# A mixture of experts: the first expert's rows by a product on TensorE, and the second expert's weights halved during routing

## What is computed

```python
scores = jax.nn.softmax((t @ w_router).astype(jnp.float32), axis=-1)
sel = scores + router_bias
...                       # best group of four, then the best two experts in it
combine = jnp.sum(jax.nn.one_hot(eidx, N_EXPERTS) * wsel[..., None], axis=1)
hg = jnp.einsum('td,edf->tef', t, w_gate)
hu = jnp.einsum('td,edf->tef', t, w_up)
h = jax.nn.silu(hg) * hu * combine[..., None]
y = jnp.einsum('tef,efd->td', h, w_down)
```

## Time and profile before

| | |
|---|---|
| median of 3 runs | 1873.3 us (1868.39 to 1873.57) |
| the profiled execution's own time | 1872.31 us |
| its span | 1870.7 us |
| mean granted TensorE clock | 0.922 of full speed |
| busy PE, DVE, ACT, POOL | 1565.5, 1221.8, 785.7, 738.5 us |
| read from HBM, written | 287.06 MB, 39.44 MB |

### The profile page before, as it was taken

The page is one execution under the profiler, slowest core; times in us unless marked ns, Lnnn a source line. Parts: engine busy times, 40 slices in busy tenths (PEclk is TensorE's granted clock), DMA queues, the critical chain, the costliest instruction groups (busy, mean ns, idle before and its releaser), DMA issues.

```text
span 1870.7 us, 27095 instructions
## 1 busy us (share of the span) xinstructions
PE 1565.5 (84%) x8954; PEld 1338.9 (72%) x8954; DVE 1221.8 (65%) x1662; ACT 785.7 (42%) x1178; POOL 738.5 (39%) x440
## 2 busy tenths in 40 slices
PE   2699899989998975999549989998999988499970
PEld 0589766679997764777438986666999967377750
DVE  0658588878937364777194947887886445477725
ACT  0422577752224132766142247776222413176621
POOL 2124399421114201887212329862111220179941
PEclk7799999999999976999869999999999989599995
DMA  7612165322212642999852205551222262479976
GB/s 289 200 45 68 53 208 203 99 58 80 68 57 91 247 156 110 342 356 338 314 187 74 68 30 181 188 163 36 68 69 78 80 247 83 178 281 353 379 268 235
DMA packets 131206, 310.06 MB, mean 166 GB/s; under 512 B 11636, under 2 KB 81396, under 8 KB 109984
## 3 DMA queue, kind: packets, MB, share of 16 engines
q1 hardware_dynamic: 104096, 224.41, 35.0%
q0 software_dynamic: 16400, 42.90, 6.1%
q10 hardware_dynamic: 10560, 40.90, 5.7%
HBM read 287.06 MB, written 39.44 MB: 175 GB/s over the span
## 4 chain that ended last, share of the span: by engine, by line
PE 62%; DMA 14%; DVE 11%; issue 7%; ACT 4%; POOL 1%; DVEq 0%; ACTq 0%; POOLq 0%; SPq 0%
PE ps L539 26%; PE ps L498 9%; PE ps L800 6%; PE ps L597 3%; PE ps L607 2%; DVE gu_lo L1498 2%; DMA raw_x<-in_w_down 2%; PE ps L454 2%; DMA raw<-in_w_down 2%; PE ps L866 2%; DMA raw<-in_w_up 2%; PE ps L586 2%; DMA raw<-in_w_ada 2%; PE ps L846 2%; PE ps L587 1%
## 5 line engine op out<-in xcount | busy, mean ns | idle before, releaser
L2279 POOL TENSOR_TENSOR w_lo<-raw,w_hi 128x1024 fp32r<-128x1024 f32 (+1 forms) x46 | 162.5, 3535 | 554.9 <-ACT w_hi L1106 554.9
L539 PE MATMUL ps<-u_hi,w_hi 128*128 128x320 f32 x768 | 238.9, 311 | 5.4 <-ACT probs L1205 5.4
L539 PE MATMUL ps<-u_lo,w_hi 128*128 128x320 f32 x768 | 238.1, 310 | 0.0
L539 PE MATMUL ps<-u_hi,w_lo 128*128 128x320 f32 x768 | 238.1, 310 | 0.0
L1106 ACT ACTIVATE w_hi<-raw 128x2048 fp32r<-128x2048 f32 (+1 forms) x64 | 101.3, 1591 | 293.7 <-PE ps L539 133.9
L1853 DVE SCALAR_TENSOR_TENSOR glu<-glu,convw 128x670 f32<-128x670 f32 x164 | 171.1, 1043 | 6.1 <-DVE o_lo L1808 0.6
L539 PEld LDWEIGHTS ps<-u_hi,w_hi 128*128 128x128 f32 x768 | 144.8, 189 | 6.0 <-ACT probs L1205 5.9
L539 PEld LDWEIGHTS ps<-u_lo,w_hi 128*128 128x128 f32 x768 | 144.8, 189 | 0.1
L539 PEld LDWEIGHTS ps<-u_hi,w_lo 128*128 128x128 f32 x768 | 144.8, 189 | 0.0
L2384 POOL DMA_INDIRECT xe<-u_d,tab_u x34 | 68.4, 2012 | 179.6 <-issue 145.2
L1713 DVE TENSOR_TENSOR pt_lo<-ps,pt_hi 128x512 fp32r<-128x512 f32 x160 | 109.7, 687 | 29.9 <-ACT pt_hi L1231 27.8
(11 more groups left out here) (379 smaller groups left out, 4254.2 us busy)
## 6 DMA issues: line engine op xcount, KB each, us to landing
raw<-in_w_ada SPq DMA_DIRECT2D x52, 1024.0 KB, 5.1
raw<-in_w_in SPq DMA_DIRECT2D x48, 512.0 KB, 5.0
raw_x<-in_w_gate SPq DMA_DIRECT2D x16, 1024.0 KB, 7.0
raw<-in_w_up SPq DMA_DIRECT2D x16, 1024.0 KB, 8.3
raw_x<-in_w_down SPq DMA_DIRECT2D x16, 1024.0 KB, 9.2
raw_x<-in_w_up SPq DMA_DIRECT2D x14, 1024.0 KB, 8.6
raw<-in_w_gate SPq DMA_DIRECT2D x14, 1024.0 KB, 6.5
raw<-in_w_down SPq DMA_DIRECT2D x14, 1024.0 KB, 9.2
```

Of the source, the lines that this page charges most:

```text
L539: ins = mm(ps[:, b, 0:HALF], (w_hi, w_lo)[w][:, s, cols(k):cols(k) + P], xs[x][:, k, half * HALF:(half + 1) * HALF], start=(k == 0 and w + ...
L2279: g_.tensor_tensor(w_lo[:, n % 2, 0:k], raw[:, n % 2, 0:k], w_hi[:, n % 2, 0:k].bitcast(F32), ALU.subtract).then_inc(*G.up("g_lo", "w_lo", n))
```

## The change

Expert 0's rows no longer come from the gather. DVE works out each token's place among expert 0's rows (2 x 640 is added where the token does not go to expert 0, so that it matches no place) and compares it with 0 to 127; the comparison matrix, 128 places for each of five tiles of tokens, is multiplied with `u2` on PE, in 8 x 5 products of full precision, into the two PSUM banks in which the transposed rows stood. The place and table products move to banks 6 and 7. `e0_gu` moves to the buffer of the projection weights, and the overflow tiles keep the old one as `over_gu`. The list of units begins with expert 2's gate and up; their high parts are made on ACT and the rests on DVE (gate) and POOL (up) between the last projection and the logits, and expert 1's down weights follow during routing. In the turn of expert 0 nothing is halved any more.

```diff
-GATE_UP_DOWN = [(1, 0), (1, 1)]
-for e in range(NE - 1):
+GATE_UP_DOWN = [(2, 0), (2, 1), (1, 0), (1, 1), (1, 2)]
+for e in range(1, NE - 1):
...
-    e0_gu = at("e0_gu", [P, 2, KC, DE], F32, R_A + 8 * KB)
+    e0_gu = at("e0_gu", [P, 2, KC, DE], F32, R_W)
+    over_gu = at("over_gu", [P, 2, KC, DE], F32, R_A + 8 * KB)
+    e0_sel = at("e0_sel", [P, NT, P], F32, R_A + 60 * KB)
+    e0_pos = at("e0_pos", [P, NT], F32, R_A + 63 * KB)
...
+            for b in range(6):
+                eng.wait_ge(*T.at("drained", last[b]))
+            eng.wait_ge(*T.at("u2", NT - 1))
+            eng.wait_ge(*T.at("e0_sel"))
+            for k in range(KC):
+                for t in range(NT):
+                    ins = mm(ps[:, k // 4, (k % 4) * P:(k % 4 + 1) * P], u2[:, t, k:D:KC], e0_sel[:, t, :], start=(t == 0), stop=(t == NT - 1))
+            ins.then_inc(*T.up("xt_full", "xt_full", 0))
+
             eng.wait_ge(*T.at("at_tile"))
-            b = fill(("table",), 1)
+            b = fill(("table",), 7)
...
-            xe_transposes(0)
...
+            eng.wait_ge(*A.at("filled", ("wo", 1, NT - 1)))
+            hi_expert(UNIT_OF[2, 0])
             ha_tr(NT - 1, 1)
             eng.dma_start(ha_d.rearrange("(t p) d -> p t d", p=P), h_a[:, :, :]).then_inc(*A.up("ha_out", "ha_out", by=16))
             eng.wait_ge(*A.at("u2", NT - 1))
             eng.dma_start(u2_d.rearrange("(t p) d -> p t d", p=P), u2[:, :, :]).then_inc(*A.up("u2_st", "u2_out", by=16))
+            hi_expert(UNIT_OF[2, 1])
...
+            eng.wait_ge(*A.at("filled", ("router",)))
+            hi_expert(UNIT_OF[1, 2])
             eng.wait_ge(*A.at("u2_out"))
-            hi_expert(UNIT_OF[1, 0])
-            hi_expert(UNIT_OF[1, 1])
...
             xt_hi_of(0)
+            hi_expert(UNIT_OF[1, 0])
+            hi_expert(UNIT_OF[1, 1])
...
-                if e + 2 < NE:
+                if 0 < e < NE - 2:
                     hi_expert(UNIT_OF[e + 2, 0])
...
+            lo(UNIT_OF[2, 0])
             eng.wait_ge(*V.at("filled", ("router",)))
...
+            v.tensor_scalar(e0_pos[:, :], cnt[:, NT - 1:, 0], -float(2 * NTOK), float(2 * NTOK), ALU.mult, ALU.add).then_inc(*V.step())
...
+            v.tensor_tensor(e0_pos[:, :], e0_pos[:, :], posp[:, :, 0], ALU.add).then_inc(*V.step())
+            eng.wait_ge(*V.at("v", V.steps))
+            v.tensor_tensor(e0_sel[:, :, :], iot128[:, :].unsqueeze(1).broadcast_to([P, NT, P]),
+                            e0_pos[:, :].unsqueeze(2).broadcast_to([P, NT, P]), ALU.is_equal).then_inc(*V.up("v_mask", "e0_sel"))
...
+            lo(UNIT_OF[2, 1])
+            lo(UNIT_OF[1, 2])
             eng.wait_ge(*G.at("tab"))
...
-            for e in range(3):
+            for e in range(1, 3):
                 gather_of(e)
```

More of the change, by code:

```diff
@@ L815, in _ @@
             eng.wait_ge(*T.at("mask"))
-            b = fill(("place",), 0)
+            b = fill(("place",), 6)
             flat = lambda x: x.rearrange("p t e -> p (t e)")
@@ L829, in _ @@
             ins.then_inc(*T.filled(("table",)))
-            for b in range(8):
-                eng.wait_ge(*T.at("drained", last[b]))
             def row_transposes(i):
@@ L861, in down, with gate_up_f @@
                 return ins
-            def gate_up_f():
+            def gate_up_f(gu):
                 for x in range(2):
                     for k in range(KC):
-                        ins = mm(ps[:, 2, x * DE:(x + 1) * DE], xt_f[:, k, :], e0_gu[:, x, k, :], start=(k == 0), stop=(k == KC - 1))
+                        ins = mm(ps[:, 2, x * DE:(x + 1) * DE], xt_f[:, k, :], gu[:, x, k, :], start=(k == 0), stop=(k == KC - 1))
                 return ins
@@ L892, in _ @@
                     eng.wait_ge(*T.at("e0_in", 1))
-                    gate_up_f().then_inc(*T.up("gu_full", "gu_full", e))
+                    gate_up_f(e0_gu).then_inc(*T.up("gu_full", "gu_full", e))
+                    for b in (6, 7):
+                        eng.wait_ge(*T.at("drained", last[b]))
                 else:
@@ L915, in _ @@
                 eng.wait_ge(sems("ov_raw1"), 16 * o)
-                gate_up_f().then_inc(sems("ov_gu"), 1)
+                gate_up_f(over_gu).then_inc(sems("ov_gu"), 1)
                 eng.wait_ge(sems("ov_h"), o)
@@ L1026, in unit, with whole @@
                 load(n, (r(n, (KC, KC, 2)[k]), io[part(k)][l, e, :, :].rearrange("(p c) n -> p c n", p=P)))
-            def first_expert(k):
-                return e0_dn[:, :, :] if k == 2 else e0_gu[:, k, :, :]
+            def whole(gu, k):
+                return e0_dn[:, :, :] if k == 2 else gu[:, k, :, :]
             for e, k in GATE_UP_DOWN[0:4]:
@@ L1035, in _ @@
             for k in range(2):
-                eng.dma_start(first_expert(k), io[part(k)][l, 0, :, :].rearrange("(p c) n -> p c n", p=P)).then_inc(*S.up(f"e0_raw{k}", "e0_in", k, by=16))
+                eng.dma_start(whole(e0_gu, k), io[part(k)][l, 0, :, :].rearrange("(p c) n -> p c n", p=P)).then_inc(*S.up(f"e0_raw{k}", "e0_in", k, by=16))
             eng.wait_ge(*S.at("u2", NT - 1))
             eng.sem_inc(sems("passed_S"), 1)
-            eng.dma_start(first_expert(2), io[part(2)][l, 0, :, :].rearrange("(p c) n -> p c n", p=P)).then_inc(*S.up("e0_raw2", "e0_in", 2, by=16))
+            eng.dma_start(whole(e0_gu, 2), io[part(2)][l, 0, :, :].rearrange("(p c) n -> p c n", p=P)).then_inc(*S.up("e0_raw2", "e0_in", 2, by=16))
             for e, k in GATE_UP_DOWN[4:]:
@@ L1054, in over @@
                     src = io[part(k)][l, bass.ds(of, 1), :, :].rearrange("a (p c) n -> p (a c) n", p=P)
-                    eng.dma_start(first_expert(k), src).then_inc(sems(f"ov_raw{k}"), 16)
+                    eng.dma_start(whole(over_gu, k), src).then_inc(sems(f"ov_raw{k}"), 16)
                 eng.wait_ge(sems("ov_gu"), o)
@@ L1414, in _ @@
                 act((ht_hi if e else ht_f)[:, :, :].rearrange("p c n -> p (c n)"), ps[:, 3, 0:2 * P], ACT.Copy).then_inc(*A.up("ht_hi", "ht_hi", e))
-                if e + 2 < NE:
+                if 0 < e < NE - 2:
                     hi_expert(UNIT_OF[e + 2, 1])
-                if e + 1 < NE:
-                    if e:
-                        eng.wait_ge(*A.at("y_full", e - 1))
+                if 0 < e < NE - 1:
+                    eng.wait_ge(*A.at("y_full", e - 1))
                     hi_expert(UNIT_OF[e + 1, 2])
@@ L2393, in gather_of @@
             def gather_of(e):
-                if e >= 2:
+                if e >= 3:
                     eng.wait_ge(*G.at("xt_full", e - 2))
```

## The result

The changed kernel takes **1880.25 us** (median of 6 runs, 1877.78 to 1883.89) against 1873.1 before (6 runs, 1868.39 to 1873.57): a ratio of **1.0045**, 95% interval 1.0031 to 1.006 (the two medians alone give 1.0038). It is slower, by a little more than the 0.3% that can be told from no change. 1853 was forecast.

A forecast was written before the change was run, and what follows sets the result against it. The prediction took the serial chain of routing, hand-over to expert 1's product and expert loop as the bound. Gains of 6.5 + 5.2 (hand-over) + 7.9 (loads) = 19.6 us led from 1872.3 to 1853, range 1838 to 1866.

The forecast's parts named there:

- the selection's price: Expert 0's selection on PE: 80 instructions at 0.23 us (1.2 GHz) or 0.1125 (2.4), taken as 11.3 us.
- The clock: PE during the selection: begins at 1.2 GHz and rises after 3 to 6 us at the lower level.
- Rival A: Clock stays at 1.2 GHz through the selection, which takes 18.4 us; kernel slower, 1868 to 1882; chance 0.12.
- forecast start of expert 1's product: Hand-over, layer 1: expert 1's product begins at 735.5 instead of 742.03, a gain of 6.5 us.
- POOL's halvings: Routing: GpSimd's halvings hold the shared port, so DVE's two-operand steps wait +2.7 and +4.2 us.
- The loads: Expert loop: three units fewer to carry, half of the possible gain taken, 4.3 and 3.6 us, together 7.9.
- rival C: Expert loop: slots, not bandwidth, set the pace, so the lead is worth nothing; 1860 to 1867; chance 0.15.
- the down weights land as forecast: Routing: expert 1's down weights, issued at about 690.7, land at about 703.8; ACT's copy ends at 705.7.
- halves leaving expert 0's turn: Expert 0's turn: the halves moved out were hidden under its product, so they gain nothing.
- forecast ahead of the loop: Hand-over up to expert 1's product: gains of 6.5 us in layer 1 and 5.2 in layer 2.

The follow-up runs named there:

- e1: Changed kernel with u2's columns written in chunk order, so selection and transposes read 128 neighbouring columns: 1870.4 us, ratio 0.9991 to the kernel before.
- e9: e6 with the table's product between the selection's sixth and seventh chunk and DVE's two halves behind the table: 1846.31 us, ratio 0.9871 to the kernel before.
- e11: e6 with PE kept busy in its two pauses by products that nothing reads: 1845.28 us, ratio 0.9869 to the kernel before.
- e6: e5 with POOL halving nothing while DVE routes; DVE does those two halves: 1852.67 us, ratio 0.9908 to the kernel before.
- e5: Changed kernel with selection reading neighbouring columns, u2 unchanged, expert 0's gate and up weights reordered to match: 1863.45 us, ratio 0.9955 to the kernel before.
- e8: Changed kernel with selection undone (gather back), new load order kept, POOL halving nothing while DVE routes: 1867.47 us, ratio 0.9976 to the kernel before.

## Why the prediction was wrong, step by step

**The step that failed is the selection's price:** "Each takes 4.60/20 = 0.23 us at 1.2 GHz and, by the row of eight of the same shape, 0.90/8 = 0.1125 at 2.4". The row of eight is the transposes'. They are of the same shape, and their stationary tile is strided in the same way, but they are one instruction each and not half of a full-precision product. Their loads in the kernel before, and in e1 where they read neighbouring columns:

```profile
L836 PEld LDWEIGHTS ps<-ident,xe x288: 184/188/232, 725.5 to 1818.2; 128*128 128x128 f32 x144
```

```profile
L845 PEld LDWEIGHTS ps<-ident,xe x272: 138/140/144, 739.9 to 1821.3; 128*128 128x128 f32 x136
```

The stride costs them 48 ns that never shows, since a transpose's step is 110 ns either way. The selection's loads went from 192 to 335, and its step at the full clock was 238 ns where 112.5 was forecast. The table's products, the other row used, load neighbouring columns. No row of the kernel before showed a full-precision product with a strided stationary tile; the two nearest rows agreed with each other and not with it. With 19.35 for 11.3 the sum moves by 8.05 a layer, 16.1 in all.

**The clock was judged right.** It rose inside the selection, 3.5 to 4.5 us after its start in layer 1 and some 5 in layer 2, within the 3 to 6 assumed. Layer 1:

```profile
712.00:714.00 2.00, 2.00 (x11) 2.00 (x9) 1.69 (x12) 0.00 (x0) 0.00 (x0) 0.50 0.00 0
...
715.00:716.00 1.00, 1.00 (x6) 1.00 (x6) 0.86 (x5) 0.00 (x0) 0.00 (x0) 1.00 0.00 0
```

Rival A's place (a selection ending after about 725) and its time (1874 to 1882) are what came, but by another cause: it wanted the clock to stay down. The Trainium skill's rule that was quoted there ("TensorE: Matmul & The Clock Gate", Part 1) agrees with these rows; the one on lines of SBUF, which speaks against this change, was not weighed.

**A second term was missing.** Expert 1's product was taken at 5.74 us. PE stood 1.88 us for the gather and 2.02 for the splits ahead of it, fell to 0.50, and the product took 7.46, and 8.30 in layer 2:

```profile
744.70:747.00 2.30, 2.29 (x5) 1.82 (x6) 0.00 (x0) 0.00 (x0) 0.00 (x0) 0.50 0.68 273
```

e9 and e11 show both ways to get this back. In layer 1 the forecast start of expert 1's product, 735.5, became 744.72: 8.05 by the selection, 0.8 by its later start (710.48 for 709.7), and the rest within 0.5.

**POOL's halvings were right:** +2.7 and +4.2 forecast, 2.65 and 4.27 measured in layer 1 (2.89 and 4.44 less the operations' own 0.24 and 0.17), 2.3 and 3.4 in layer 2. The second hit the sum of the two weights in layer 1 and the comparison in layer 2 (4.24 us for 0.83). Small operations do wait as long as wide ones, by these rows and by the Trainium skill's rule that the prediction quotes ("SBUF — State Buffer", "SBUF: two separate sides"). Without the halvings on POOL (e6) the selection starts 6.2 and 5.7 us sooner after the logits than in the changed kernel, where 6.9 was forecast; e5 to e6, the total falls by 10.8 us.

**The loads were put too high.** 4.3 and 3.6 were forecast. The marks of one profile say 4.3 and -0.9. Over two profiles of the kernel before and thirteen of kernels with the new order, layer 1 gained 2.9 (138.2 to 135.3) and layer 2 lost 0.8 (135.2 to 136.0): some 2 of 7.9. SP's queue shows why. The seventh and the tenth load of the changed kernel:

```profile
735.03 0.33 SPq L997 DMA_DIRECT2D raw<-in_w_up  x1
...
760.31 0.33 SPq L997 DMA_DIRECT2D raw_x<-in_w_up  x1
```

and the tenth before:

```profile
755.90 0.33 SPq L987 DMA_DIRECT2D raw_x<-in_w_up  x1
```

The seventh is 9.8 us earlier than in the earlier trace rows. The tenth is issued 8.10 us after expert 1's SiLU now, and was 8.09 after it before: it needs a raw buffer that is free only when expert 3's gate weights are halved (DVE ends that at 760.28), and their halves go where expert 1's lie until its product is done. The lead ends there, as rival C said, and three loads of lead could not be kept. e8, the new order alone, gained 0.24% (interval 0.07 to 0.4%), most of it ahead of the loop (2.6 and 1.0 us at expert 1's SiLU against one profile of the kernel before, 1.2 and 2.3 against the other). That the down weights land as forecast (copy of ACT to 704.25, 705.7 forecast) and that halves leaving expert 0's turn cost nothing fits; the latter was not tried alone.

Put together, by marks: -6.5 and -5.2 forecast ahead of the loop against +4.1 and +5.3, and -7.9 in the loops against -3.4. The selection's 16.1, the 4.3 that expert 1's product lost in two layers and the 4.5 of the loops come to 24.9; the profiled execution is 24.8 above the forecast, and what is left cancels. Without the stride (e5) the kernel would have stood at 1863, inside the forecast range but 10 us above its 1853.

## What to carry to other kernels

Price an operation by a row with the same operand layout in the same kind of instruction: a stride that one instruction hides sets the pace of another. If the stationary tile of a full-precision product must be read with a stride, keep two elements in each 16 bytes, or put the permutation where it is free, here into the order in which weights are loaded. Work moved onto POOL beside a chain of small DVE operations costs each of its whole durations, not a share; and where PE waits a few microseconds ahead of a long product, look at what the pause does to the product as well.

## What the runs showed of the hardware

- A weight load of 128x128 for a full-precision float32 product takes 192, 196, 330 and 335 ns at distances of 4, 8, 16 and 32 bytes and a granted clock of 1.00. The step of the product is then 112, 118, 233 and 238 ns. At 0.50 the loads take 333, 331, 330 and 338 and the steps are 213, 213, 233 and 240, so the load of every fourth or eighth column does not follow the clock.
- On DVE, an addition of 128x1024 in float32 takes 2.02 us with 32 bytes between the elements of one of its two inputs, 1.23 without.
- In e6 two pauses of PE, 2.24 us for the gather and 2.21 for the splits with transposes (1.16 and 0.40 us) between them, stood ahead of a fall of the clock: 1.00 while the transposes ran, 0.50 for 4 us of the product behind them. In e11, with products in both pauses, that product ran at the full clock.

```profile
728.30:729.50 1.20, 1.12 (x10) 1.12 (x10) 0.00 (x0) 0.00 (x0) 0.00 (x0) 1.00 0.94 365
729.50:732.00 2.50, 0.28 (x4) 0.10 (x2) 1.23 (x1) 1.30 (x2) 0.99 (x1) 0.60 1.04 405
732.00:736.00 4.00, 4.00 (x10) 3.13 (x11) 0.00 (x0) 0.00 (x0) 0.00 (x0) 0.50 0.52 206
```

- An operation of 5 columns on DVE waited 4.27 us for a POOL operation of 2048; its own width is 0.17.
